# A transformer block pair on one core: the opening's first norm, its last two quarters, the order of its weight loads and of three sums

## The reference

```
mod = silu(c) @ w_ada + b_ada                  # 2048 x 12288
shift_m, scale_m, gate_m, shift_f, scale_f, gate_f = split(mod, 6)
h = rms_norm(x, pre_norm_mix) * (1 + scale_m) + shift_m
q, k, v, gates ... = split(h @ w_in)            # 2048 x 5656
o = [nsa_mixer(...), moba_mixer(...)]           # two kinds of attention, 8 heads each
x = x + gate_m * rms_norm(o @ w_o, post_norm_mix)
...                                             # MLP of the first block, then the second block
```

## Time and profile before

| | us |
|---|---|
| median of three runs | 2958.68 |
| the profiled execution's own time | 2958.95 |
| its span (first to last instruction) | 2956.8 |
| PE busy in the span | 2874.6 |
| DVE busy | 1701.4 |
| ACT busy | 1254.4 |

### The profile page before, as it was taken

One profiled execution on the slowest core, in us unless ns is written; L12 is line 12 of the kernel. 1 busy time (PEld: TensorE's weight loads), 2 busy tenths in 40 slices (PEclk: granted clock), 3 DMA queues, 4 the chain that ended last, 5 costly groups with the idle time before them and its releaser, 6 DMA issues.

```text
span 2956.8 us, 50977 instructions
## 1 busy us (share of the span) xinstructions
PE 2874.6 (97%) x22328; PEld 2652.0 (90%) x22328; DVE 1701.4 (58%) x1507; ACT 1254.4 (42%) x1197; POOL 130.3 (4%) x111
## 2 busy tenths in 40 slices
PE   6999999999999999999999999999999999999998
PEld 5899987799889997899999889999979998899887
DVE  7879877795444454455455654445745554455444
ACT  3334444444434543345343544443345443344333
POOL 0011110000000000000022320000000000000000
PEclk8799999999999999999999999999999999999999
DMA  9999778596556655655452016566554555565553
GB/s 360 388 317 305 268 238 297 176 368 225 186 198 188 197 190 180 203 191 175 157 168 66 10 45 199 187 197 221 178 185 159 197 187 197 187 197 189 181 194 119
DMA packets 300452, 596.72 MB, mean 202 GB/s; under 512 B 12144, under 2 KB 17776, under 8 KB 299760
## 3 DMA queue, kind: packets, MB, share of 16 engines
q1 hardware_dynamic: 294864, 587.83, 59.1%
q10 hardware_dynamic: 5408, 6.23, 0.8%
HBM read 583.80 MB, written 6.29 MB: 200 GB/s over the span
## 4 chain that ended last, share of the span: by engine, by line
PE 83%; DVE 8%; DMA 3%; ACT 3%; issue 2%; POOL 0%; SPq 0%; ACTq 0%; DVEq 0%
PE ps L2429 30%; PE ps L2352 26%; PE ps L2949 9%; PE ps L2534 4%; DVE ada_acc L1593 3%; PE ps L2549 3%; DVE wL L1373 2%; PE ps L3072 2%; DMA ada<-w_ada 2%; PE ps L2830 2%; ACT wH L770 1%; PE ps L2510 1%; DMA raw<-w_up 1%; PE ps L2375 1%; PE ps L2331 0%
## 5 line engine op out<-in xcount | busy, mean ns | idle before, releaser
L1373 DVE TENSOR_TENSOR wL<-raw,wH 128x2048 fp32r<-128x2048 f32 x436 | 1004.3, 2304 | 1064.1 <-ACT wH L770 1060.0
L770 ACT ACTIVATE wH<-raw 128x2048 fp32r<-128x2048 f32 x436 | 837.8, 1922 | 1277.7 <-PE ps L2429 475.4
L2429 PE MATMUL ps<-actH,wH 128*128 128x256 f32 x2816 | 779.3, 277 | 1.7 <-DVE wL L1373 1.6
L2429 PE MATMUL ps<-actL,wH 128*128 128x256 f32 x2816 | 777.7, 276 | 0.0
L2429 PE MATMUL ps<-actH,wL 128*128 128x256 f32 x2816 | 777.7, 276 | 0.0
L2429 PEld LDWEIGHTS ps<-actH,wH 128*128 128x128 f32 x2816 | 529.0, 188 | 3.9 <-DVE wL L1373 2.1
L2429 PEld LDWEIGHTS ps<-actL,wH 128*128 128x128 f32 x2816 | 529.0, 188 | 0.1
L2429 PEld LDWEIGHTS ps<-actH,wL 128*128 128x128 f32 x2816 | 528.9, 188 | 0.0
L2352 PE MATMUL ps<-wH,hidH 128*128 128x512 f32 x1024 | 403.4, 394 | 1.3 <-DVE wL L1373 1.3
L2352 PE MATMUL ps<-wH,hidL 128*128 128x512 f32 x1024 | 400.4, 391 | 0.0
L2352 PE MATMUL ps<-wL,hidH 128*128 128x512 f32 x1024 | 397.4, 388 | 0.0
(11 more groups left out here) (438 smaller groups left out, 3654.6 us busy)
## 6 DMA issues: line engine op xcount, KB each, us to landing
raw<-w_in SPq DMA_DIRECT2D x96, 1024.0 KB, 5.3
ada<-w_ada SPq DMA_DIRECT2D x80, 1024.0 KB, 8.3
raw<-w_up SPq DMA_DIRECT2D x64, 1024.0 KB, 5.4
raw<-w_down SPq DMA_DIRECT2D x64, 1024.0 KB, 5.1
raw<-w_mlp_up SPq DMA_DIRECT2D x64, 1024.0 KB, 5.2
raw<-w_mlp_down SPq DMA_DIRECT2D x64, 1024.0 KB, 5.0
raw<-w_gates SPq DMA_DIRECT2D x48, 1024.0 KB, 5.1
raw<-w_o SPq DMA_DIRECT2D x16, 1024.0 KB, 6.5
```

The lines of the kernel that those rows point to most:

```text
L770: nc.scalar.activation(wH[:, s % SPLIT if L[name]["spg"] > 1 else r % SPLIT, :, :], raw[:, slot, :, :], ACT.Copy).then_inc(wh_ready, 1)
L1373: nc.vector.tensor_tensor(wL[:, b, :, :], raw[:, slot, :, :], wH[:, b, :, :].bitcast(F32), ALU.subtract).then_inc(wl_ready, 1)
L2429: ins = nc.tensor.matmul(out, w[:, b, k, cols], v[:, kk, :], start=(kk == 0 and j == 0 and n % 2 == 0), stop=(kk == STEP_K * spg - 1 and j ...
```

## The change

It has these parts:

- the first norm: PE transposes x first; ACT copies it out token-major and squares it there with an accumulated sum (two instructions of 128 x 2048), takes the root of 128 x 2, DVE inverts 128 x 2, ACT builds two 128 x 128 diagonals, and PE writes x back feature-major and normalised as x times the diagonal (32 float32 matmuls of 128 x 128), which ACT copies to `x_f`. `over_root` is gone, and the two warm-up matmuls fewer;
- the coefficients of quarters 1 and 2 come behind one ada block of DVE instead of two;
- quarters 2 and 3 are made a tile at a time: ACT makes `actH` from `x_f` directly, DVE splits tile by tile, block 9 is split in two halves, PE waits for tiles and halves;
- `gate_part(c)` runs before `front_total(2c+3)`, and two matmuls that nothing reads come after the latter;
- SP's order: the front's blocks 0 to 2 one ada block earlier, blocks 9 to 12 behind ada block 31 and before the spill; then 13, 14, posk, 15, ada 32, cw1 (k), 16, ada 33, cw1 (v), cw2;
- `WIN_ADA[0]` goes from (2, 0, 0, 1) to (0, 0, 1, 2): DVE sums ada 32 after split 14, and 33 and 34 after split 15.

```diff
-    WIN_ADA = [(2, 0, 0, 1), (1, 1, 3, 4), (1, 1, 0, 1)] + [(2, 1, 0, 1)] * 4 + [(2, 1, 0, 2)]
+    WIN_ADA = [(0, 0, 1, 2), (1, 1, 3, 4), (1, 1, 0, 1)] + [(2, 1, 0, 1)] * 4 + [(2, 1, 0, 2)]
...
# SP
-                    if c == 0 and n >= 5:
-                        weight_block(n - 5)
+                    if c == 0 and n in (4, 5, 6):
+                        weight_block(n - 4)
...
-                    if c == 3 and n == 2:
-                        weight_block(FRONT * c)
+            weight_block(FRONT * 3)
             weight_block(FRONT * 3 + 1)
+            weight_block(FRONT * 3 + 2)
+            weight_block(FRONT * 3 + 3)
             sp.wait_ge(xT_out, 2 * (KT // GT))
             sp.dma_start(a["out"]...).then_inc(x_spill, 16)
-            weight_block(FRONT * 3 + 2)
             sp.dma_start(c1[:, :], a["c1"]).then_inc(c1_in, 16)
-            weight_block(FRONT * 3 + 3)
             weight_block(9 + RAW)
+            weight_block(10 + RAW)
+            sp.wait_ge(ada_sum, STEP_K * NFRONT)
+            sp.wait_ge(ada_rows, NFRONT // 4)
+            sp.dma_start(posk[:, :, :], a["pos"]).then_inc(pos_in, 16)
+            weight_block(11 + RAW)
             ada_block(NFRONT)
+            sp.dma_start(cw1[:, 0, :, :], ...).then_inc(cmp_in, 16)
+            weight_block(12 + RAW)
             ada_block(NFRONT + 1)
-            sp.wait_ge(ada_sum, STEP_K * NFRONT)
-            ...
-            weight_block(10 + RAW)
-            ...
-            weight_block(11 + RAW)
# ACT
-            for c in range(KT // GT):
-                nc.scalar.activation(... sq ..., ... x_f ..., ACT.Square).then_inc(sq_ready, 1)
-            act.wait_ge(ssum_ready, 1)
-            nc.scalar.activation(std[:, :], ps[:, 6, 0:T], ACT.Sqrt, bias=eps, scale=1.0 / D).then_inc(std_ready, 1)
             for n in range(2 * (KT // GT)):
                 ...
+                if c == KT // GT - 1:
+                    act.wait_ge(xT_out, n + 1)
+                    chain(nc.scalar.activation(sq_tok[:, t, :], x[:, t, :], ACT.Square, accum_out=rms[:, 1, t:t + 1]))
+            nc.scalar.activation(rms[:, 0, :], rms[:, 1, :], ACT.Sqrt, bias=eps, scale=1.0 / D).then_inc(std_ready, 1)
+            act.wait_ge(low_part, 1)
+            for t in range(TT):
+                ins = nc.scalar.activation(rstd_d[:, t, :], ident, ACT.Identity, scale=rms[:, 2, t:t + 1])
+            ins.then_inc(high_part, 1)
+            for n in range(2 * (KT // GT)):
+                act.wait_ge(xT_done, 2 * (KT // GT) + n + 1)
+                nc.scalar.activation(flat(x_f[:, 2 * n:2 * n + 2, :]), ps[:, n % 4, :], ACT.Copy).then_inc(xT_out, 1)
...
+                if c >= 2:
+                    ...
+                    for k in range(GT):
+                        n = GT * c + k
+                        ins = nc.scalar.activation(actH[:, n, :], x_f[:, n, :], ACT.Identity, bias=mod[:, 0, n:n + 1],
+                                                   scale=cf(0)[:, n:n + 1])
+                        if k:
+                            ins = nc.scalar.activation(yf[:, c % 2, k, :], x_f[:, n, :], ACT.Identity, ...)
# DVE
-                    if c == 0 and n == 6:
-                        over_root(0)
-                    if c and n == (c > 1):
+                    if c == 0 and n == 5:
+                        dve.wait_ge(std_ready, 1)
+                        nc.vector.reciprocal(rms[:, 2, :], rms[:, 0, :]).then_inc(low_part, 1)
+                    if c and n == 0:
                         front_coefficients(c - 1)
-                        front_split(c - 1, 0)
-                        front_low(c - 1)
+                        if c == 3:
+                            first_low(2)
+                            front_split(2, 0)
+                            rest_low(2)
+                        else:
+                            front_split(c - 1, 0)
+                            front_low(c - 1)
...
-                    if c and n == 5:
-                        over_root(c)
-            front_split(3, 0)
+            dve.wait_ge(high_part, 4)
+            dve.wait_ge(step_done, FRONT * 3 + 1)
+            last_half(slice(0, 2), low_part)
             front_coefficients(3)
-            front_low(3)
+            first_low(3)
+            dve.wait_ge(wh_ready, FRONT * 3 + 1)
+            last_half(slice(2, 4), wl_ready)
+            rest_low(3)
...
-            ada_blocks(1)
             split("w_in", 0, 0, 0)
-            ada_blocks(1)
+            split("w_in", 0, 0, 1)
             rope(0)
-            split("w_in", 0, 0, 1)
             compress_inputs()
             split("w_in", 0, 0, 2)
+            ada_blocks(1)
             rope_sin(1)
             rope_sum(1)
             split("w_in", 0, 0, 3)
-            ada_blocks(1)
+            ada_blocks(2)
# PE
-                    ins = nc.tensor.matmul(ps[:, 6, 0:T], ones, sq[:, k, :], start=(k == 0), stop=(k == KT - 1))
...
+            def unread(n):
+                for _ in range(n):
+                    nc.tensor.matmul(ps[:, 7, P:P + T], ident, common[:, 0:T], start=False, stop=False, skip_group_check=True)
             front_total(0)
+            pe.wait_ge(high_part, 1)
+            for n in range(2 * (KT // GT)):
+                ...
+                for j in range(4):
+                    k, t = 2 * n + j // 2, j % 2
+                    ins = nc.tensor.matmul(ps[:, n % 4, j * P:(j + 1) * P], x[:, t, k * P:(k + 1) * P], rstd_d[:, t, :],
+                                           start=True, stop=True)
+                ins.then_inc(xT_done, 1)
+            pe.wait_ge(xT_out, 4 * (KT // GT))
             front_total(1)
...
-                if c < 3:
-                    front_total(2 * c + 3)
                 if c == 0:
                     pe.wait_ge(gw_lo, 1)
                 ins = gate_part(c)
+                if c < 3:
+                    front_total(2 * c + 3)
+                if c < 3:
+                    unread(2)
```

More of the change, by code:

```diff
@@ L241, in build_program @@
     sq = at("sq", [P, KT, T], F32, R0)
+    sq_tok = at("sq_tok", [P, TT, D], F32, R0)
     K1 = 1024
@@ L1649, in front_coefficients, with piece_low, first_low, rest_low @@
                                                ).then_inc(coef_ready, 1)
+            def piece_low(c, k):
+                n = GT * c + k
+                nc.vector.tensor_tensor(actL[:, n, :], yf[:, c % 2, k, :], actH[:, n, :].bitcast(F32), ALU.subtract
+                                        ).then_inc(act_ready if k % 2 else low_part, 1)
+            def first_low(c):
+                n = GT * c
+                dve.wait_ge(coef_ready, c + 1)
+                link(nc.vector.tensor_scalar(yf[:, c % 2, 0, :], x_f[:, n, :], cf(0)[:, n:n + 1], mod[:, 0, n:n + 1], ALU.mult, ALU.add))
+                dve.wait_ge(high_part, 2 if c == 2 else 5)
+                piece_low(c, 0)
+            def rest_low(c):
+                dve.wait_ge(h_ready, 2 * c + 1)
+                piece_low(c, 1)
+                dve.wait_ge(high_part, 3 if c == 2 else 6)
+                piece_low(c, 2)
+                dve.wait_ge(h_ready, 2 * c + 2)
+                piece_low(c, 3)
             for c in range(KT // STEP_K):
@@ L2447, in _ @@
             pe.wait_ge(consts_in, 48)
-            for _ in range(4):
+            for _ in range(2):
                 nc.tensor.matmul(ps[:, 4, :], ident, common[:, 0:4 * P], start=True, stop=True)
-            for c in range(KT // GT):
-                pe.wait_ge(sq_ready, c + 1)
-                for k in range(GT * c, GT * (c + 1)):
-                    ins = nc.tensor.matmul(ps[:, 6, 0:T], ones, sq[:, k, :], start=(k == 0), stop=(k == KT - 1))
-            ins.then_inc(ssum_ready, 1)
+            pe.wait_ge(x_in, 16)
             for n in range(2 * (KT // GT)):
@@ L2500, in _ @@
                     l = FRONT * c + n
-                    pe.wait_ge(wl_ready, RAW + l + 1)
+                    last = c == 3 and n == 0
+                    pe.wait_ge(wl_ready, RAW + l + 1 - last)
                     for k in range(STEP_K):
                         kk = c * STEP_K + k
-                        if n == 0 and k % 2 == 0:
+                        if n == 0 and k % 2 == 0 and c < 2:
+                            pe.wait_ge(act_ready, kk // 2 + 1)
+                        if n == 0 and k % 2 == 0 and c >= 2:
+                            pe.wait_ge(low_part, (2 if c == 2 else 5) + k // 2)
+                        if last and k == 2:
+                            pe.wait_ge(wl_ready, RAW + l + 1)
+                        if n == 0 and k % 2 and c >= 2:
                             pe.wait_ge(act_ready, kk // 2 + 1)
```

52 lines of the change are left out of this document (34 added, 18 removed).

## The result

The changed kernel takes **2984.86 us** (median of 18 runs, 2976.38 to 2991.67), the kernel before 2962.51 in the same session (18 runs): ratio 1.0072, 95% interval 1.0063 to 1.0082. It is 22 us slower. Forecast were 2963.4 with a range of 2954 to 2968, so the measurement lies outside, on the side of the forecast but five times as far; none of the three rivals reached beyond 2968 either. The profiled execution has a span of 2981.8 against 2956.8, 25.0 more.

A forecast was written before the change was run, and what follows sets the result against it. PE's unbroken run from 135 us sets the end, by its start and waits; DVE and transfers are full in the opening. Group 1 +6.0, lost PE wait -1.3: +4.7 on 2958.95 gives 2963.6, 2963.4 against the median; range 2954 to 2968.

The forecast's parts named there:

- The first norm: Opening: the new chain's root ends at 27.1 us, first coefficients come at 42.5 instead of 41.47, up to 46 at low clock.
- What the norm moves: Opening: DVE's saved 3.0 us are spent waiting; quarter 0 starts 1.3 us earlier; 3.7 us of later products go.
- Coefficients behind one block: Quarters 1 and 2: 1.4 us of DVE wait each, 2.8 in all; bounds 0.2 and 1.8 each.
- The finer quarters: Quarters 2 and 3: 0.9 us more on DVE, last ada sum at 133.7, PE's last quarter at 138.4, 4.5 us earlier.
- The order: Before group 1: ada 34 lands at 190 (186 to 193), so group 1 starts at 195.1, 6.0 us later.
- The waits expected: DVE waits 5 to 10 us for w_ada, PE 8 to 12 before group 1; the 1.3 us wait near 241 goes.
- Rival A: Before group 1: the wait for ada 34 eats the early start; +2 to +8 us, 2961 to 2967; chance 0.55.
- rival B: Before group 1: ada 34 lands by about 184, not slower; -3 us, 2956.0, chance 0.27; 2954 or less, another 0.05.
- Rival C: First norm: products and total stay at low clock, coefficients at 46, group 1 at 198 to 200; 2968 us; chance 0.13.

The follow-up runs named there:

- norm_alone_gate_late: Kernel before with the new first norm alone, w_gate's load issued behind the last copy of x_f; 2957.40 us, ratio 0.9991.
- _early: Kernel before with the new first norm alone, w_gate's load issued behind the root; 2956.71 us, ratio 0.9981.
- gate_early: Changed kernel with w_gate's load issued behind the first norm's root instead of the last copy of x_f; 2977.64 us, ratio 1.0049.
- mended_one_block: Changed kernel with w_gate's load early, sums and loads in the old order, coefficients still behind one ada block; 2961.21 us, ratio 0.9999.
- mended_two_blocks: Changed kernel with w_gate's load early, sums and loads in the old order, coefficients behind two ada blocks; 2957.29 us, ratio 0.9992.
- two_sums_blocks_early: Changed kernel with ada 32 and 33 sent for behind block 13, no longer behind blocks 15 and 16; 2973.67 us, ratio 1.0041.
- before_with_new_order: Kernel before with sums of ada 32 to 34 put off and loads from block 9 on in the changed order; 2986.90 us, ratio 1.0079.
- all_but_norm_and_finer_undone: Changed kernel keeping only the new first norm and finer quarters, w_gate's load early, the rest as before; 2956.29 us, ratio 0.9977.
- mended_sums_put_off: all_but_norm_and_finer_undone with the changed sums and loads, but ada 32 and 33 sent for behind block 13; 2965.58 us, ratio 1.0015.

## Why the prediction was wrong, step by step

**The first norm: right.** Root at 27.0 (forecast 27.1), coefficients of quarter 0 at 41.83 (42.5), DVE idle 4.99 before them (4 to 5), quarter 0 on PE at 45.2 (45.6, by its 1.3 us). Of the drain behind a table load that the Trainium skill states (ScalarE: Activation LUTs, What ACT_TABLE_LOAD costs), this row shows nothing: ACT's instruction before the load ends at 25.69, the load runs from 25.71 to 26.99, and the root starts at 27.01.

**What the norm moves: missed.** The prediction followed the new chain on ACT to its last copy and not the instruction behind it, the issue of w_gate's load, which slid from 29.9 to 39.8. The copy of w_gate is in front of block 2's copy in ACT's program. "DVE's 3.0 us are therefore spent waiting. What comes back ... quarter 0 starts 1.3 us earlier" is as far as it went; 5.7 us of DVE wait came 17 us later. norm_alone_gate_late against _early and gate_early show it: 3.2 us at the last quarter with coefficients behind two blocks, 8.3 behind one. Of the forecast for the last ada sum, 133.7, the measured 141.9 is 8.2 us off, and ada 31 went out at 131.9 instead of near 123.5.

**Coefficients behind one block: right in kind, too small.** Forecast: 1.4 us of wait for each of quarters 1 and 2. The wait rows are 4.25 and 1.80, and the third split of a quarter now stands ahead of the ada block that PE's total waits for (1.71 and 1.70 in the PE rows). With gate early one block costs 2.4 to 3.8 us at the last quarter (141.3 in gate_early and 142.7 in mended_one_block, against 138.9), where the forecast had 2.8; with gate late 7.1 (149.6 against 142.5).

**The finer quarters: right where the gate part is out of the way**, 4.45 us from the start of the total to the quarter (forecast 4.7 from the last ada sum, 0.14 of it ahead of the total). The opening that the prediction described exists: mended_two_blocks has the last quarter at 138.9, the forecast was 138.4. It contains neither the late load nor the one-block coefficients. The forecast's sum has the one-block coefficients in it and knew no late load, and a kernel with neither meets it: that the number agrees is in part luck. And the last quarter is no earlier there than with the new norm alone (138.7), so at that point the finer quarters gained nothing that shows.

**The order: the step that failed.** "The queue is full in this stretch, so what counts is how much stands before it ... 34 lands at 190." The share of 1.06 belonged to the old order. The step counted bytes ahead of ada 34 and not the state of SP, which is held by a raw slot, and by the issue of cw2, with free ada slots behind it. Its 190 became 204.2 in the changed kernel, and 198.1 on the opening of before. Nor did it count the wait for the spill of x, which stands in SP's program ahead of ada 32 beside the wait for the slot and was 5.7 us long in two_sums_blocks_early. On the very opening of before the term came out at 23.1 us (before_with_new_order) where 6.0 were set against it. The Trainium skill's ceiling of 435 GB/s (DMA: Bandwidth & Descriptors, Where 436 GB/s comes from), weighed there as a rival, was not reached in any stretch shown: 380 is the most here, and 381 in the earlier trace rows. The same section of the Trainium skill calls 435 the ceiling of the ports and says that transfers from the chip's memory are bound at some 358; the prediction left that out. The measured 380 and 381, in stretches at shares of 1.03 and 1.05, lie above it, and the measurement decides.

**The waits expected: right in kind, too short.** DVE waited 10.85 us for w_ada (5 to 10), released by a transfer, and PE 14.86 (8 to 12), released by DVE, both some 20 us later than they were placed. The 1.3 us of wait in the earlier trace rows are gone as said. Rival A's mechanism is what happened; rival B, with 0.27, is out: at 204.2 ada 34 was 20 us over its bound of 184. Rival C's low clock came, but behind the waits and not in the first norm. All three rivals, with nearly all of the chance, ended at 2968: what was missing among them was a wait of SP.

**Open.** In the mended opening the change from all_but_norm_and_finer_undone to mended_sums_put_off is 9.3 us of median (12.7 by the distance to before), and the put-off sums alone cost 3.0 on the kernel before. What the other 6 to 10 us are, the place of blocks 9 to 12, of cw1, or the two together, isn't settled. The spill behind blocks 9 to 12 is one candidate, with the 4.5 us that SP waits for it there; no run moved the spill alone. Nor is it settled how much of the 2.7 us lost behind the start of group 1 is the lower clock: group 1's first step takes 7.1 us there instead of 5.8.

## What to carry to other kernels

A queue that is full in the profile is full in its present order: before moving a load, list what the issuing engine itself waits for in front of it, and which slots stand free meanwhile. When a stage is lengthened on an in-order engine, follow that engine's program one issue and one wait further than the stage's last result. And make each part's gain in a kernel of its own: here the new norm by itself gave 3.7 us, and the order of the loads by itself, a few moved lines, took 22.

## What the runs showed of the hardware

Issues of transfers held SP for 8 to 13 us when a half of cw1 (2 MB) had been issued shortly before: 12.64 for the 64 KB of cw2, 8.21 for block 16 behind the first half, against 0.4 for a block otherwise. The kernel before has it too: 9.60 for the second half of cw1 and 8.65 for cw2, with ada 32 and 33 already sent. No run tells whether it is the number or the size of the rows that does it.

PE's matmuls stayed at the low clock (1.2 GHz; 0.41 us a matmul against 0.28, a total of 16 in 3.54 against 1.92 us) for a time behind its gaps of 5.80 and of 14.86 us. They did so behind one of 1.70 at 132.04 too, and behind one of 1.71 at 98.88 only from 101.7 to 105.1 us. In the kernel before the low clock came at 215.5 with no gap ahead of it, behind 8 us of products with 30 columns and with one. The stretch from 204 to 260 was granted 0.71 instead of 0.85, and 7.4 us of it are the gap itself. The long wait was thus followed by a step 1.3 us longer than before; that a gap of a given length costs so much is not shown.
